# The recurrence's up-projection moved between the samples' value products of an earlier stage, with a ring of 6 places

## The reference

```python
def merge_ffn(x, o_lru, o_nsa, o_mem, merge, p):
    z = (merge[:, :, 0] * (o_lru @ p['w_up_a']) + merge[:, :, 1] * (o_nsa @ p['w_up_b'])
         + merge[:, :, 2] * (o_mem @ p['w_up_m']))
    h = x + z @ p['w_o']
    f = rmsnorm(h, p['norm_ffn'])
    return h + (jax.nn.silu(f @ p['w_ffn_gate']) * (f @ p['w_ffn_up'])) @ p['w_ffn_down']
```

## Time and profile before

| | |
|---|---|
| median of 3 runs | 2627.57 us (2626.29 to 2628.66) |
| the profiled execution's own time | 2635.17 us |
| its span, first to last instruction | 2633.5 us |
| TensorE busy | 2423.0 us, 92% of the span |
| `memory_and_samples`, TensorE's first to last matmul | 1353.8 to 1563.5 us |
| `tail`, first matmul to the end of the 16 up units | 1577.5 to 1769.0 us |
| `tail`, the rest | 1769.0 to the end |

### The profile page before, as it was taken

How to read it: one execution, slowest core, us unless ns; L and a number is a source line. 1 busy time by engine, 2 the same in 40 slices (tenths; PEclk the granted TensorE clock), 3 DMA queues, 4 the chain that set the end, 5 groups by cost and what they waited for, 6 DMA issues and landing times. The chain is left out here.

```text
span 2633.5 us, 37761 instructions
## 1 busy us (share of the span) xinstructions
PE 2423.0 (92%) x14399; PEld 2240.0 (85%) x14399; DVE 1067.0 (41%) x1945; ACT 721.1 (27%) x1319; POOL 652.7 (25%) x390
## 2 busy tenths in 40 slices
PE   7997777989989989899967979999999999999999
PEld 7996547878889788889844778999999999999999
DVE  5465013435345374555433103353233333333333
ACT  5222011233243544644433004222211111111111
POOL 2112101112211011011013101234443344343343
PEclk9997689999999999999778759999999999999999
DMA  5223516225523131111036315322111111111112
GB/s 180 89 81 124 174 36 181 70 71 176 132 74 112 39 107 47 55 61 32 13 97 199 116 59 207 120 91 103 58 49 40 48 48 40 48 48 40 48 48 80
DMA packets 135963, 226.31 MB, mean 86 GB/s; under 512 B 30842, under 2 KB 93946, under 8 KB 135228
## 3 DMA queue, kind: packets, MB, share of 16 engines
q1 hardware_dynamic: 119612, 196.75, 23.7%
q0 software_dynamic: 5376, 21.00, 2.3%
q10 hardware_dynamic: 10848, 6.82, 0.9%
HBM read 176.80 MB, written 55.08 MB: 88 GB/s over the span
## 5 line engine op out<-in xcount | busy, mean ns | idle before, releaser
L1114 PE MATMUL att_facc<-h_hi,att_w_hi 128*128 128x344 f32 x960 | 338.5, 353 | 58.6 <-DVE att_zf L1294 45.2
L2149 PE MATMUL tl_acc<-tl_x_hi,tl_w_hi 128*128 128x344 f32 x1632 | 347.9, 322 | 21.3 <-DVE tl_x_lo L2212 14.5
L2149 PE MATMUL tl_acc<-tl_x_lo,tl_w_hi 128*128 128x344 f32 x1632 | 347.1, 321 | 0.0
L2149 PE MATMUL tl_acc<-tl_x_hi,tl_w_lo 128*128 128x344 f32 x1632 | 345.4, 320 | 0.0
L1114 PE MATMUL att_facc<-h_lo,att_w_hi 128*128 128x344 f32 x960 | 315.6, 329 | 0.0
L1114 PE MATMUL att_facc<-h_hi,att_w_lo 128*128 128x344 f32 x960 | 315.5, 329 | 0.0
L2149 PEld LDWEIGHTS tl_acc<-tl_x_hi,tl_w_hi 128*128 128x128 f32 x1632 | 275.0, 189 | 22.9 <-issue 15.9
L2149 PEld LDWEIGHTS tl_acc<-tl_x_lo,tl_w_hi 128*128 128x128 f32 x1632 | 276.9, 189 | 0.0
L2149 PEld LDWEIGHTS tl_acc<-tl_x_hi,tl_w_lo 128*128 128x128 f32 x1632 | 272.6, 188 | 0.0
L2114 POOL TENSOR_TENSOR tl_w_lo<-tl_raw,tl_w_hi 128x1024 fp32r<-128x1024 f32 x64 | 154.2, 2409 | 424.4 <-ACT tl_w_hi L2055 424.4
L1114 PEld LDWEIGHTS att_facc<-h_hi,att_w_hi 128*128 128x128 f32 x960 | 188.6, 196 | 73.1 <-DVE att_zf L1294 42.8
(11 more groups left out here) (352 smaller groups left out, 3997.5 us busy)
## 6 DMA issues: line engine op xcount, KB each, us to landing
tl_raw<-in_w_ff SPq DMA_DIRECT2D x66, 512.0 KB, 3.5
z<-att_zf SPq DMA_DIRECT2D x120, 172.0 KB, 3.9
att_raw<-in_w_in SPq DMA_DIRECT2D x40, 512.0 KB, 4.0
tl_tmp<-z SPq DMA_DIRECT2D x24, 516.0 KB, 4.3
tl_raw<-in_w_up SPq DMA_DIRECT2D x16, 512.0 KB, 4.1
fr_raw<-in_w_in SPq DMA_DIRECT2D x14, 512.0 KB, 4.7
zn<-fr_x SPq DMA_DIRECT2D x10, 516.0 KB, 2.9
fr_x<-in_xT SPq DMA_DIRECT2D x8, 644.0 KB, 10.3
```

Source lines behind the costliest of these rows:

```text
L1114: mm = pe.matmul(facc[:, 0:CW], w[:, u % 2, k, :], h[:, k, c * CW:(c + 1) * CW], start=(x == 0), stop=(x == 23))
L2149: mm = pe.matmul(a[:, c, 0:CW], wt[:, s, k, :], x[:, x0, c * CW:(c + 1) * CW], start=first and n == 0, stop=last and n == 2)
```

## The change

The eight units of `w_up` that multiply `o_lru` leave `tail` and run in `memory_and_samples` as a filler of 96 ticks of 6 matmuls: 6 ticks after each `sample_values(b)` and 6 after each `memory_values(b)`, none in the other parts. A group is 24 matmuls (4 ticks: one chunk of 344 columns) into one bank `facc`, which VectorE copies to `z`, ungated. For it, `o_lru` is loaded to `z` at the start (8 DMAs on SyncE's queue, ahead of the samples' constants and ring), ScalarE makes its high parts after tiles 2 to 9, GpSimd its low parts ahead of its share of the ring loads; weights are loaded on ScalarE's queue, their high parts are ScalarE's and their low parts VectorE's. Two units ahead are prepared, so the first two units of `tail` are ready when it begins. The buffers are taken from `ring`, which has 6 places instead of 24. In `tail`, z holds the recurrence's product; `gated_recurrence` multiplies it by its gate in place; x blocks and gates share the 5 places of `tmp`.

The core of the diff:

```diff
-    NR, NJ = 24, MH * QT
+    NR, NJ = 6, MH * QT
...
+    DEAL = {"mat": 0, "ks": 0, "grp": 0, "km": 0, "turn": 0, "vs": 6, "vm": 6}
+    chunks = {p: [t // 4 for t in ticks[p] if t % 4 == 3] for p in points}
+    whole = {p: [t // 12 for t in ticks[p] if t % 12 == 11] for p in points}
+    loads = {points[points.index(p) + 1]: [u + 4 for u in whole[p] if u + 4 < KT + 2] for p in points[:-1]}
...
+            for k in range(KT):
+                sp.dma_start(z[:, k], d["o_lru"][k]).then_inc(x_in[k], 16)
             constants(0)
-            for i in range(0, 10, 2):
+            for i in range(0, NR, 2):
                 ring_load(sp, i)
             for b in range(1, NS):
                 constants(b)
-            for i in range(10, len(ITEMS), 2):
+            for i in range(NR, len(ITEMS), 2):
                 ring_load(sp, i)
...
         @block.gpsimd
+            for k in range(KT):
+                pool.wait_ge(xu_hi, k + 1)
+                pool.tensor_tensor(x_lo[:, k], z[:, k], x_hi[:, k].bitcast(F32), ALU.subtract).then_inc(xu_lo, 1)
             for i in range(1, len(ITEMS), 2):
                 ring_load(pool, i)
...
+            def filler(p):
+                for tick in ticks[p]:
+                    u, c, g, x0 = tick // 12, tick // 4 % 3, tick // 4, 6 * (tick % 4)
+                    if tick % 12 == 0:
+                        pe.wait_ge(f_lo, u + 1)
+                    if x0 == 0 and g:
+                        pe.wait_ge(f_ev, g)
+                    for x in range(x0, x0 + 6):
+                        k = x // 3
+                        w, h = ((w_hi, x_hi), (w_hi, x_lo), (w_lo, x_hi))[x % 3]
+                        mm = pe.matmul(facc[:, 0:CW], w[:, u % 2, k, :], h[:, k, c * CW:(c + 1) * CW],
+                                       start=(x == 0), stop=(x == 23))
+                    if x0 == 18:
+                        mm.then_inc(f_mm, 1)
...
             for b in range(NS):
                 sample_values(b)
+                filler(("vs", b))
...
             for b in range(NS):
                 memory_values(b)
+                filler(("vm", b))
...
+            def weights(p):
+                for u in loads.get(p, ()):
+                    w_load(u)
+                for u in whole[p]:
+                    w_high(u + 2)
...
+                if j in (1, 2):
+                    w_high(j - 1)
+                if 2 <= j < KT + 2:
+                    x_high(j - 2)
...
+            def evict(p):
+                for g in chunks[p]:
+                    u, c = g // 3, g % 3
+                    dve.wait_ge(f_mm, g + 1)
+                    dve.tensor_copy(z[:, u, c * CW:(c + 1) * CW], facc[:, 0:CW]).then_inc(f_ev, 1)
+                for u in whole[p]:
+                    w_low(u + 2)
...
+            for b in range(NS):
+                evict(("vs", b))
             dve.wait_ge(o_mm, NS)
...
+            for b in range(NS):
+                evict(("vm", b))
             dve.wait_ge(mo_mm, NS)
...
     def tail
-    U_O, U_F, G_O, G_F = 16, 24, 24, 32
+    U_O, U_F, G_O, G_F = 8, 16, 16, 24
...
+            def gated_recurrence(m):
+                dve.wait_ge(sg_done, 3 * m + 1)
+                dve.tensor_tensor(z[:, m], z[:, m], place(KT + 3 * m)[0], ALU.mult).then_inc(mul_done, 1)
...
+            for k in range(KT):
+                x_part(k)
             for m in range(KT):
+                gated_recurrence(m)
+                gated(m, 1)
+                gated(m, 2)
```

More of the change, by code:

```diff
@@ L1418, in _, with memory_and_samples @@
                     evict(g)
-def memory_and_samples(nc, d, per):
+def memory_and_samples(nc, d, per, up):
+    x_hi, x_lo, raw, w_hi, w_lo, z = up
     SC = P ** -0.5
-    NR, NJ = 24, MH * QT
+    NR, NJ = 6, MH * QT
     RW, RM, RP = NS * 8, NS * MH, 64
     LS, LW, NB = NP_ + 1, WIN + 1, 16
+    points = [("mat", j) for j in range(NJ)] + [("ks", b) for b in range(NS)] + [("grp", 0)]
+    points += [("km", b) for b in range(NS)] + [("turn", 0)] + [("vs", b) for b in range(NS)] + [("vm", b) for b in range(NS)]
+    DEAL = {"mat": 0, "ks": 0, "grp": 0, "km": 0, "turn": 0, "vs": 6, "vm": 6}
+    ticks, done = {}, 0
+    for p in points:
+        n = 0 if p[0] == "mat" and p[1] < 10 else DEAL[p[0]]
+        ticks[p] = list(range(done, done + n))
+        done += n
+    assert done == 12 * KT
+    chunks = {p: [t // 4 for t in ticks[p] if t % 4 == 3] for p in points}
+    whole = {p: [t // 12 for t in ticks[p] if t % 12 == 11] for p in points}
+    loads = {points[points.index(p) + 1]: [u + 4 for u in whole[p] if u + 4 < KT + 2] for p in points[:-1]}
     ITEMS = []
@@ L1479, in memory_and_samples @@
         mS, mtp, mO = bank[1:4]
+        facc = bank[7]
+        x_in = [sem(f"x_in{k}") for k in range(KT)]
+        u_in = [sem("u_in0"), sem("u_in1")]
+        xu_hi, xu_lo, f_hi, f_lo, f_mm, f_ev = (sem(x) for x in ("xu_hi", "xu_lo", "f_hi", "f_lo", "f_mm", "f_ev"))
         m_in, pt_in = sem("m_in"), sem("pt_in")
@@ L1658, in _ @@
                 turn(j)
+                filler(("mat", j))
             values(NJ - 1)
@@ L1665, in _ @@
                 sample_scores(b)
+                filler(("ks", b))
             pe.wait_ge(s_oe, NJ)
@@ L1672, in _ @@
                 memory_scores(b)
+                filler(("km", b))
             pe.wait_ge(w_done, 1)
@@ L1798, in _ @@
                     memory_queries((j - 18) // 2)
+            evict(("mat", NJ - 1))
+            for b in range(NS - 1):
+                evict(("ks", b))
             dve.wait_ge(k_mm, NS)
@@ L1834, in _ @@
             dve.tensor_reduce(sc[:, 2:3], ls[:, 0:LS], AX, ALU.max, negate=True).then_inc(a_done, 1)
+            for b in range(3):
+                evict(("km", b))
             dve.wait_ge(g_mm, 1)
@@ L1843, in _ @@
             dve.tensor_scalar(ls[:, 0:LS], ls[:, 0:LS], sc[:, 9:10], gt[:, 1:2], ALU.mult, ALU.mult).then_inc(w_done, 1)
+            for b in range(3, NS):
+                evict(("km", b))
             dve.wait_ge(mk_mm, NS)
@@ L1881, in tail @@
         wr_in = [sem("wr_in0"), sem("wr_in1")]
-        x_in = [sem(f"x_in{s}") for s in range(NST)]
-        mg_in = [sem(f"mg_in{s}") for s in range(NMG)]
+        t_in = [sem(f"t_in{s}") for s in range(NST)]
+        mul_done = sem("mul_done")
         h_in = [sem(f"h_in{k}") for k in range(KT)]
@@ L1951, in _, with t_load @@
-            for k in range(2, 8):
-                x_load(k)
-            mg_load(0)
+            def t_load(n):
+                slot, landed, _ = place(n)
+                if NST <= n < KT + NST:
+                    sp.wait_ge(xlo_done, n - NST + 1)
+                elif n >= KT + NST:
+                    m, b = (n - NST - KT) // 3, (n - NST - KT) % 3
+                    if b == 0:
+                        sp.wait_ge(mul_done, m + 1)
+                    else:
+                        sp.wait_ge(add_done, 2 * m + b)
+                sp.dma_start(slot, branches[n] if n < KT else d["z"][U_MG + 8 * ((n - KT) % 3) + (n - KT) // 3]).then_inc(landed, 16)
@@ L1964, in _ @@
+            for u in range(4, U_O + 2):
                 w_load(u)
[L1965 to L1968 removed]
+                for n in range(3 * u - 7, 3 * u - 4):
                     if n < 3 * KT:
[L1970 removed]
+                        t_load(KT + n)
+            t_load(4 * KT - 1)
             w_load(U_O + 2)
@@ L2154, in _ @@
             for u in range(U_O):
-                for k0, nk, x0 in ((0, KT, 0),) if u < KT else ((0, 4, 8), (4, 4, 12)):
+                for k0 in (0, 4):
                     pe.wait_ge(wlo_done, u + 1)
@@ L2304, in program @@
             attention_and_recurrence(nc, d, per, h_hi, h_lo)
-        memory_and_samples(nc, d, per)
-        tail(nc, d, per)
+        with ExitStack() as part:
+            sbu = sb_of(nc, part, "up")
+            up = (sbu("x_hi", [P, KT, T], F32R), sbu("x_lo", [P, KT, T], F32R), sbu("raw", [P, 2, KT, P]),
+                  sbu("w_hi", [P, 2, KT, P], F32R), sbu("w_lo", [P, 2, KT, P], F32R), sbu("z", [P, KT, T]))
+            memory_and_samples(nc, d, per, up)
+            tail(nc, d, per, up)
 def _bucket(n):
```

202 lines of the change are left out of this document (98 added, 104 removed).

## The result

The changed kernel takes 2651.80 us (median of 3 runs, 2648.02 to 2655.79) against 2627.57: ratio 1.0092, interval 1.0075 to 1.0110, slower by 24 us. The forecast was 2642, the range 2622 to 2662. The profiled execution took 2655.79 us, its span 2654.1.

What follows compares the result with a forecast made beforehand. TensorE was taken to bound the kernel: busy at clock 0.50 on weight-bound passes in the samples' values, at 1.00 in the tail. Terms summed to +14.6 us on the 2627.6 median: 2642, range 2622 to 2662 (own range 2632 to 2656).

Steps and rivals of the forecast that it cites:

- the clock over the samples' values: Sign in the changed profile: granted clock 0.8 to 0.95 there, 0.95 or more over the memory's values.
- rival 3: Clock lost for most of each dense stretch behind a sample's values: 37 us instead of 9, 2670 us; chance 0.15.
- a wait for a gate: Sign that the prediction is wrong: the tail's first groups wait for gates; a returning wait was put at 5.5 us.
- The tail: Tail loses 576 matmuls; its 16 remaining up groups take 93 us instead of 191.5, first matmul 2 sooner: -100.5 us.
- The filler's own price: The same 576 matmuls, run in the samples' stage at 0.158 us each: +90.9 us.
- Falls of the clock: Over the samples' values, six falls at 1.5 us each: +9 us, bounds 0 and 24; two further restarts +3.
- rival 1: The clock stays up in the whole of the values, so the falls vanish (-9): 2633 us; chance 0.22.
- The copies: Emptying the filler's one bank inside samples: 16 exposed copies at 0.81 us each, +13 us (11 to 15).
- The ring: Six places pause sample 6's scores for loads, +18.6 us, and the first values, +3.9; S is the scores' start.
- Rival 2: Later samples' pages issue faster, so both load pauses (18.6 + 3.9) go: 2620 us; chance 0.13.
- The memory tiles: GpSimd's eight low parts in tiles 2 to 11 delay VectorE's multiplication, over 1 us some eight times: +8 us (2 to 18).
- Between the two kinds of values: TensorE's 0.5 us idle there grows as VectorE first empties a bank and makes a weight's low part: +2.7 us.

Runs made afterwards that it cites:

- the profile where thin and dense work are mixed and the other losses gone: Changed kernel with ring items in tile z, two filler banks, low parts on VectorE, and filler ticks inside the samples' values: 2596.18 us, ratio 0.9879.
- the ring of 6 alone: Kernel before the change with one edit, 6 ring places instead of 24, no filler or early loads: 2655.18 us, ratio 1.0098.
- the low parts on VectorE: Changed kernel with o_lru's eight low parts made on VectorE in halves behind tiles 4 to 19, not on GpSimd: 2647.51 us, ratio 1.0075.
- keys in `z`: Changed kernel with ring items 6 to 11 and 18 to 23 placed in the idle tile z: 2633.41 us, ratio 1.0009.
- places, banks and VectorE: Changed kernel with ring items in tile z, two filler banks and low parts on VectorE: 2609.51 us, ratio 0.9927.
- the second run: Unchanged repeat of the changed kernel with ring items in the tile z: 2631.61 us, ratio 1.0008.

## Why the prediction was right, and where its terms were off

The sign, the range and the places of the losses held: the faster thin passes, the copies and the pauses of the ring are there, and the tail gains what it should. The sizes did less well: the sum in the changed stretches was 14.6 where 28.2 was measured, and four of the six stretches came out dearer than forecast. That 2651.8 still lies inside the forecast's own range (2632 to 2656) is in part luck: the 5.0 that the smaller ring gave back in the tiles was not in the sum, and without it the time would be near 2657. Of the signs named ahead, three came otherwise: the clock over the samples' values was 0.76, between the 0.8 to 0.95 that was expected and the 0.5 to 0.6 of rival 3; the multiplication of the tiles lasted over 1 us twice and not eight times; and a wait for a gate, named as a sign that the prediction is wrong, did come in the tail, though a short one. Point by point:

- *The tail*, -98.5 forecast, -96.6 measured. Most of what differs is one wait for the gates, 1.49 us at 1709.31 on VectorE's gate multiplication (L2318), which the prediction had named as a risk, with a bound of 5.5.
- *The filler's own price*, +90.9, is the pace of 0.158 us again wherever the clock is up.
- *Falls of the clock* is the term that was mis-sized most. I took six falls at 1.5 us, from a restart in the tail that needed 9 slow matmuls. There were four, but they cost 14.44, 13.18, 14.41 and 14.52 less 10.16 each, 15.9 in all, 4.0 each; some 15 to 28 low matmuls stand behind each fall. The first sample has 5.7 more than 10.16 where 3.3 and a restart of 1.5 were counted. So the step that was off is the price of a fall: the restart in the tail came behind 5.5 us of idleness, and behind thin work the clock stayed low for longer. The bounds, 0 to 24, held it. Rival 3 (the clock lost for most of each dense stretch) is wrong for the memory's values (0.98) and three samples (1.00), and near the truth for the others; rival 1 (the clock stays up) is wrong in this kernel, and comes true in the profile where thin and dense work are mixed and the other losses gone (1.00 over the samples' values).
- *The copies*, 0.81 each forecast. The timeline gives 0.93 us from the last matmul before a copy to the first behind it, less the 0.158 of a slot, and 0.10 that the first then takes longer: 0.87, 14 in all. (The forecast's sum takes 0.50 for the copy where the earlier trace rows has 0.52; with that it is 0.83.)
- *The ring*, +18.6 and +3.9 forecast, +23.0 and +5.2 measured. The mechanism was right, the places of the waits too. I let GpSimd begin at S + 6.8; it began at S + 9.6. Half of that is the first sample, which took 5.3 us from a low clock where I had taken 3.9 from before; the other half is that the first page went out 1.6 us after the second sample ended at S + 8.0, where the sum left 0.2. Its 16 pages then took 1.5 us each as forecast, the window keys landed 3.8 after their issue, sample 6 began at S + 38.0 in place of S + 34.7, and it took 5.1 itself. The same lag shows before the first values: from the third sample's memory scores (S + 58.6) to the landing it took 16.4 where the sum has 15.0. (Its S + 54.3 fits the 8.0 us that those three took in the trace of before; the 16.79 for 8 that it names would give S + 52.4.) Rival 2 (the loads keep up) is wrong: a page took 1.5 us on GpSimd's queue here too.
- *The memory tiles*, +8 forecast, +3.4 measured, is a price of the right size beside a gain that I did not see. Against the ring of 6 alone the tiles lose 8.4; but the smaller ring first gave back 5.0, by loading less under them. I had called the loads "nothing, or 3". The price came in another form than foretold, though: two multiplications lasted over 1 us (1.59 and 2.25), not eight, and 3.3 of the 8.4 stay with the low parts on VectorE. So its size is in part luck.
- *Between the two kinds of values* the wait is 2.80 us, 2.3 more than the 0.50 of the earlier trace rows; 2.7 more was forecast.

So where the forecast has 81.6 for the values, 92.4 were measured. Falls and restarts are 6.7 of the difference: 115 low matmuls at 0.129 more each, 14.8, and thin passes of 47.8 us by their starts in place of 43.9, together 18.7 for the 12 forecast. The copies are 0.9, and the first matmul behind each of 16 thin runs, which takes 0.1 longer, 1.6; the pause between the two kinds gives back 0.5. Some 2 are not assigned.

What stays open: what decides, with thin and dense work in blocks, in which samples the clock falls. Two profiles of one kernel differ by 40 low matmuls and 7 us, and the changed kernel differs from the first profile with keys in `z` by 68. The wait before the first value does not explain it: with places, banks and VectorE that wait is 1.43 too, and there are 110 low matmuls.

## What to carry to other kernels

Dense work moved between weight-bound work can buy the clock, and the order counts: here 16 thin passes (1.7 us) at a time, with 36 dense matmuls between, kept 0.98, 30 (3.5 us) let it fall in some samples, and 4 to 6 at a time with 6 dense matmuls kept 0.97 and 1.00. Put it every few passes rather than in blocks, and give it two banks. When a buffer is shrunk to make room, price the first consumer that outruns the loads, and look for a tile that is idle at that time before paying with ring places. And check whether the larger buffer was worth its traffic at all.

## What the hardware showed that was not expected

A VectorE multiplication that meets an unbroken row of GpSimd subtractions can be held not for one of them but for all eight: 17.75 and 18.35 us in two runs, for 0.35 us of work. The row of the second run (instructions, min/median/max in ns):

```profile
L1880 DVE TENSOR_SCALAR sam_pr<-sam_pr,sam_rs x32: 352/353/18346, 1350.7 to 1441.3; 128x256 f32<-128x256 f32 x32
```

In the changed kernel, where ScalarE's copies space most of the subtractions, the longest was 2.25. Spacing is not the whole reason, though. The first two subtractions there follow each other without a pause, and the multiplication that meets the first of them is over in 1.59:

```profile
1357.16 4.87 POOL L1603 TENSOR_TENSOR up_x_lo<-up_z,up_x_hi 128x1032 fp32r<-128x1032 f32 x2 [59.02 <-ACT up_x_hi L1779]
1358.21 1.59 DVE L1871 TENSOR_SCALAR sam_pr<-sam_pr,sam_rs 128x256 f32<-128x256 f32 x1
```

What lets VectorE in between two subtractions was not shown.

The granted clock over the same order of instructions, the samples' values, was 0.94 in one execution of a kernel (1487.32 to 1573.45) and 0.82 in the next profile of it (1490.80 to 1586.90, 10.0 us longer). Such a schedule also scatters: 2622.8 to 2639.2 us over 11 runs.
